# Depthwise convolution taps on TensorE for two output tokens at a time, in a two-block float32 transformer kernel

## The reference

```
q, k = rope(rms_norm(q)), rope(rms_norm(k))          # 8 heads of 64
attn = softmax(q @ k.T / 8, causal) @ v              # 256 tokens: one block
a, g = split(u + glu_b)
h    = pad(a * sigmoid(g), 30 rows in front)
conv[t, c] = sum_{j=0..30} dw_w[j, c] * h[t + j, c] + dw_b[c]     # 512 channels
conv = silu(layer_norm(conv) * ln_g + ln_b)
x    = x + concat(attn, conv) @ w_out
x    = x + (silu(h2 @ w_gate) * (h2 @ w_up)) @ w_down             # h2 = rms_norm(x)
```

## Time and profile before

| | us |
|---|---|
| median of three runs | 756.14 (755.87 to 756.16) |
| the profiled execution | 756.11 |
| its span in the trace | 754.3 |
| PE busy | 749.9, 99% of the span |
| DVE busy | 568.5, 75% |
| ACT busy | 400.9, 53% |
| POOL busy | 50.8, 7% |

### The profile page before, as it was taken

How to read it: one execution, slowest core, us unless ns; L and a number is a source line. 1 busy time by engine, 2 the same in 40 slices (tenths; PEclk the granted TensorE clock), 3 DMA queues, 4 the chain that set the end, 5 groups by cost and what they waited for, 6 DMA issues and landing times.

```text
span 754.3 us, 9798 instructions
## 1 busy us (share of the span) xinstructions
PE 749.9 (99%) x3820; PEld 620.8 (82%) x3820; DVE 568.5 (75%) x908; ACT 400.9 (53%) x524; POOL 50.8 (7%) x39
## 2 busy tenths in 40 slices
PE   9999999999999999999999999999999999999998
PEld 7888899888888888888888888887688888888887
DVE  6869789986767877687788748697658777768584
ACT  6765455646567546546555455655556344343430
POOL 0200000000002400000000000732000000000000
PEclk9999999999999999999999999999999999999999
DMA  9963434555363467565655575677034756565601
GB/s 313 386 221 95 157 120 161 195 169 162 117 219 116 167 212 261 182 219 175 218 179 178 200 222 206 227 188 271 2 113 147 244 179 211 171 210 177 222 3 56
DMA packets 71101, 137.12 MB, mean 182 GB/s; under 512 B 3216, under 2 KB 9232, under 8 KB 70928
## 3 DMA queue, kind: packets, MB, share of 16 engines
q1 hardware_dynamic: 70448, 136.37, 54.4%
q10 hardware_dynamic: 608, 0.14, 0.1%
HBM read 133.12 MB, written 1.05 MB: 178 GB/s over the span
## 4 chain that ended last, share of the span: by engine, by line
PE 95%; DVE 3%; ACT 1%; issue 1%; DVEq 0%; ACTq 0%
PE b L698 21%; PE b L700 21%; PE b L699 21%; PE SS L698 4%; PE SS L700 4%; PE SS L699 4%; PE TT L665 3%; PE OO L698 3%; PE OO L700 3%; PE OO L699 3%; DVE wlo L1668 1%; PE OO L1041 1%; PE b L871 1%; PE SS L817 1%; PE b L1041 1%; PE SS L835 1%
## 5 line engine op out<-in xcount | busy, mean ns | idle before, releaser
L1668 DVE TENSOR_TENSOR wlo<-raw,whi 128x2048 fp32r<-128x2048 f32 (+2 forms) x119 | 270.2, 2273 | 80.8 <-ACT whi L1205 80.1
L1205 ACT CAST whi<-raw 128x2048 fp32r<-128x2048 f32 (+2 forms) x119 | 222.9, 1878 | 124.3 <-PE b L700 85.9
L698 PE MATMUL b<-whi,Ahi 128*128 128x512 f32 (+2 forms) x520 | 204.0, 392 | 0.0
L700 PE MATMUL b<-whi,Alo 128*128 128x512 f32 (+2 forms) x520 | 199.5, 384 | 0.0
L699 PE MATMUL b<-wlo,Ahi 128*128 128x512 f32 (+2 forms) x520 | 199.3, 383 | 0.0
L700 PEld LDWEIGHTS b<-whi,Alo 128*128 128x128 f32 x520 | 97.9, 188 | 19.5
L698 PEld LDWEIGHTS b<-whi,Ahi 128*128 128x128 f32 x520 | 98.1, 189 | 18.6 <-ACT gates L1289 0.2
L699 PEld LDWEIGHTS b<-wlo,Ahi 128*128 128x128 f32 x520 | 98.1, 189 | 18.1
L2087 DVE STREAM_TRANSPOSE hT<-ust 32x256 f32<-32x256 f32 (+1 forms) x192 | 81.5, 425 | 2.7
L698 PE MATMUL b<-whi,Bhi 128*128 128x512 f32 x154 | 60.4, 392 | 0.1
L700 PE MATMUL b<-whi,Blo 128*128 128x512 f32 x154 | 60.0, 389 | 0.0
(11 more groups left out here) (311 smaller groups left out, 1023.2 us busy)
## 6 DMA issues: line engine op xcount, KB each, us to landing
raw<-in_w_in SPq DMA_DIRECT2D x38, 1024.0 KB, 5.1
raw<-in_w_up SPq DMA_DIRECT2D x16, 1024.0 KB, 5.4
raw<-in_w_dn SPq DMA_DIRECT2D x16, 1024.0 KB, 5.0
raw<-in_w_d SPq DMA_DIRECT2D x11, 1024.0 KB, 5.0
raw<-in_w_g SPq DMA_DIRECT2D x10, 1024.0 KB, 5.1
raw<-in_w_u SPq DMA_DIRECT2D x10, 1024.0 KB, 5.1
raw<-in_w_out SPq DMA_DIRECT2D x8, 1024.0 KB, 5.4
raw<-in_w_br SPq DMA_DIRECT2D x4, 1024.0 KB, 5.2
```

The lines of the kernel that those rows point to most:

```text
L698: e.matmul(dst, xh, H[:, kc, c0:ce], start=(first or c0 == 768) and kc == krs[0], stop=False)
L700: ins = e.matmul(dst, xl, H[:, kc, c0:ce], start=False, stop=last and kc == krs[-1])
L1205: e.copy(whi[:, s, 0:m], raw[:, r, 0:m]).then_inc(s_hi, 1)
L1668: e.tensor_tensor(wlo[:, s, 0:m], raw[:, r, 0:m], whi[:, s, 0:m].bitcast(F32), ALU.subtract).then_inc(s_lo, 1)
```

## The change

All taps go to PE, and a matmul makes two neighbouring output tokens at a time. The input `ch` is stored with even and odd tokens apart; `hs` has 8 shifts of 16 channels in its 128 partitions; a weight tile of 32 columns holds 16 channels for each of the 2 output phases; a matmul has 128 columns (token pairs). There are 8 outputs of 4 steps, 32 steps, 256 records. `hs` is filled through DRAM: 8 transfers of `ch` to an internal tensor, a wait for them, then 8 transfers of 140-element rows into `hs`. The second set stands one weight unit later in SP's list. DVE does no taps, and there are two `taps_out` of four outputs each. The attention's row sums come from a column of ones beside each head of V instead of `accum_out`; `aw` takes its reciprocals from the product's bank after it is done. `S2` has four buffers. The order of `az`, `ap`, tap steps and `at` stays. The layer norm has the token phases interleaved in each bank, so it takes four bn_stats of 256 elements and four subtract-multiplies of 256, and both turns back wait for all of them. Lists of steps: 6, then 9, 5, 5, 4, then 2, 1, 0.

```diff
-        tw = sb("tw", [128, 128 * len(TAPS)], c=r3)
-        hs = sb("hs", [128, 4 * NTE, 288], c=r3)
+        tw = sb("tw", [128, 4096], c=r3)
+        hs = sb("hs", [128, 8, 4, 144], c=r3)
...
-        ch = sb("ch", [128, 4, 288], c=g2)
+        ch = sb("ch", [128, 4, 2, 144], c=g2)
...
-        S2 = sb("S2", [128, 3, 384], c=g2)
-        V2 = sb("V2", [128, 2, 512], c=g2)
+        S2 = sb("S2", [128, 4, 384], c=g2)
+        V2 = sb("V2", [128, 2, 8, 72], c=g2)
...
+    shifts = nc.dram_tensor("shifts", [16, 8, 1152], F32, kind="Internal").ap()
...
             if i == unit_of["wo2", 0, 1, 0]:
                 w.wait_ge(s_ug, 2)
-                for g in range(4):
-                    for s in range(4):
-                        e.dma_start(hs[32 * s:32 * s + 32, NTE * g:NTE * g + NTE, 0:284],
-                                    ch[32 * g:32 * g + 32, :, s:s + 284]).then_inc(d_hs, 16)
+                for q in range(8):
+                    e.dma_start(shifts[:, q, :], ch[16 * q:16 * q + 16].rearrange("p k r u -> p (k r u)")).then_inc(d_ch, 16)
+            if i == unit_of["wo2", 0, 1, 0] + 1:
+                w.wait_ge(d_ch, 128)
+                for s in range(8):
+                    src = shifts.rearrange("c q (k r u) -> c (q k) r u", k=4, r=2)
+                    e.dma_start(hs[16 * s:16 * s + 16, :, :, 0:140].rearrange("p q k u -> p (q k) u"),
+                                src[:, :, s % 2, s // 2:s // 2 + 140]).then_inc(d_hs, 16)
             load(i)
...
         def conv(m):
-            o, j = TAPS[m]
-            bk, c = TAPB[o % 2], 256 * (o // 2)
+            o, j = m // 4, m % 4
+            bk, c = TAPB[o // 4], 128 * (o % 4)
...
             for g in range(4):
-                ins = e.matmul(bank[bk][32 * g:32 * g + 32, c:c + 256],
-                               tw[:, 32 * (4 * m + g):32 * (4 * m + g) + 32],
-                               hs[:, NTE * g + TILE[o], 4 * j:4 * j + 256], start=j == 0, stop=last)
+                ins = e.matmul(bank[bk][32 * g:32 * g + 32, c:c + 128], tw[:, 32 * (4 * m + g):32 * (4 * m + g) + 32],
+                               hs[:, 4 * (o % 2) + g, o // 2, 4 * j:4 * j + 128], start=j == 0, stop=j == 3)
...
-                        ins = e.matmul(bank[bk][64 * c:64 * c + 64, 128 * qb + 64 * i:128 * qb + 64 * i + 64],
-                                       PT2[:, i, a:a + 64], V2[:, kb, 64 * h:64 * h + 64], start=kb == 0, stop=kb == qb)
+                        o = 72 * (2 * qb + i)
+                        ins = e.matmul(bank[bk][64 * c:64 * c + 64, o:o + 65], PT2[:, i, a:a + 64], V2[:, kb, h, 0:65],
+                                       start=kb == 0, stop=kb == qb)
...
-        tile_parts(3)
+        tile_parts(6)
         for p in range(4):
             az(p)
             if p:
                 ap(p - 1)
-            tile_parts((7, 5, 5, 4)[p])
+            tile_parts((9, 5, 5, 4)[p])
             at(p)
         tile_parts(2)
         ap(3)
...
-        tile_parts(1)
+        tile_parts(0)
...
         def ln_turn(p):
             bk = NBK[p]
             clear(bk)
-            w.wait_ge(s_cf, NTE)
-            for k in range(4):
-                ins = e.transpose(bank[bk][:, 128 * k:128 * k + 128], cdv[:, k, 128 * p:128 * p + 128], ident)
-            ins.then_inc(s_l1, 1)
+            w.wait_ge(s_cf, p + 1)
+            turn4(bank[bk], cdv[:, 4 * p:4 * p + 4, :].rearrange("p o u -> p (o u)")).then_inc(s_l1, 1)
         def ln_back(p):
-            w.wait_ge(s_lv, p + 1)
+            w.wait_ge(s_lv, 2)
...
-            e.activation(P[:, 0:128], P[:, 0:128], ACT.Exp, bias=nm[:, 0:1], scale=-1.0, accum_out=l[:, 0:1])
-            e.activation(P[:, 128:384], P[:, 128:384], ACT.Exp, bias=nm[:, 1:2], scale=-1.0,
-                         accum_out=l[:, 1:2]).then_inc(s_ae, 1)
+            e.activation(P[:, 0:128], P[:, 0:128], ACT.Exp, bias=nm[:, 0:1], scale=-1.0)
+            e.activation(P[:, 128:384], P[:, 128:384], ACT.Exp, bias=nm[:, 1:2], scale=-1.0).then_inc(s_ae, 1)
...
+        def taps_out(b):
+            w.wait_ge(s_cp, b + 1)
+            e.tensor_tensor(cdv[:, 4 * b:4 * b + 4, :], bank[TAPB[b]].rearrange("p (o u) -> p o u", o=4),
+                            pcol("dw_b", 4 * b, 4).unsqueeze(2).broadcast_to([128, 4, 128]), ALU.add).then_inc(s_cf, 1)
...
         def aw(p):
-            w.wait_ge(s_ae, 2 * p + 2)
-            k = own(e.reciprocal(l, l))
+            o = bank[p % 2][:, 0:288].rearrange("p (q h d) -> p q h d", q=2, h=2)
+            l = sums[:, 4 * p:4 * p + 4].rearrange("p (q h) -> p q h", q=2)
+            w.wait_ge(s_ap, p + 1)
             w.wait_ge(s_ut, 4)
-            w.wait_ge(s_ap, p + 1)
+            k = own(e.reciprocal(l, o[:, :, :, 64]))
...
         for p in range(4):
             am(2 * p)
             am(2 * p + 1)
+            if p == 1:
+                taps_out(0)
             if p:
                 aw(p - 1)
-            conv((2, 2, 2, 2)[p])
-            if p in {1: 0, 2: 1, 3: 2}:
-                taps_out({1: 0, 2: 1, 3: 2}[p])
...
         def ln():
+            rows = [[bank[NBK[j]].rearrange("p (g r c) -> p r g c", r=2, c=16)[:, p] for j in range(2)] for p in range(2)]
+            for j in range(2):
+                w.wait_ge(s_l1, j + 1)
+                for p in range(2):
+                    k = own(e.bn_stats(bs[p][:, 6 * j:6 * j + 6], rows[p][j]))
             for p in range(2):
-                w.wait_ge(s_l1, p + 1)
-                k = own(e.bn_stats(bs[p], bank[NBK[p]]))
...
             for p in range(2):
                 w.wait_ge(s_rs, RS[f"l{p}"] + 1)
-                e.tensor_scalar(ys[:, p, 512:1024], bank[NBK[p]], mv[p][:, 0:1], lnr[p], ALU.subtract,
-                                ALU.mult).then_inc(s_lv, 1)
+                for j in range(2):
+                    ins = e.tensor_scalar(ys[:, p, 512 + 256 * j:768 + 256 * j].rearrange("p (g c) -> p g c", c=16),
+                                          rows[p][j], mv[p][:, 0:1], lnr[p], ALU.subtract, ALU.mult)
+                ins.then_inc(s_lv, 1)
```

More of the change, by code:

```diff
@@ L71 @@
       18: (33, 34, 35, 36), 20: (41, 42, 43, 44), 22: (45, 46, 47, 48)}
[L73 to L76, removed]
 CH2 = [(2048, 512), (1536, 512), (0, 512), (512, 512), (1024, 512)]
@@ L462, in build @@
     rp8, rpv, rpr = [stat(8) for _ in range(4)], [stat(8) for _ in range(4)], [stat(8) for _ in range(4)]
-    bs, mv, lnv, lnr = [[stat(n) for _ in range(2)] for n in (6, 2, 1, 1)]
+    mv, lnv, lnr = [[stat(n) for _ in range(2)] for n in (2, 1, 1)]
+    bs = [lscr[:, 16 * i:16 * i + 12] for i in range(2)]
     r1c, r1cq = rpv[3][:, 0:4:2], rpv[3][:, 1:4:2]
@@ L1030, in conv @@
         def conv(m):
-            o, j = TAPS[m]
-            bk, c = TAPB[o % 2], 256 * (o // 2)
+            o, j = m // 4, m % 4
+            bk, c = TAPB[o // 4], 128 * (o % 4)
             if m == 0:
-                w.wait_ge(d_hs, 256)
+                w.wait_ge(d_hs, 128)
                 w.wait_ge(d_tw, 32)
-            if j == 0:
+            if m % 16 == 0:
                 clear(bk)
-            last = (o, j + 1) not in TAPS
             for g in range(4):
-                ins = e.matmul(bank[bk][32 * g:32 * g + 32, c:c + 256],
-                               tw[:, 32 * (4 * m + g):32 * (4 * m + g) + 32],
-                               hs[:, NTE * g + TILE[o], 4 * j:4 * j + 256], start=j == 0, stop=last)
-            if last:
+                ins = e.matmul(bank[bk][32 * g:32 * g + 32, c:c + 128], tw[:, 32 * (4 * m + g):32 * (4 * m + g) + 32],
+                               hs[:, 4 * (o % 2) + g, o // 2, 4 * j:4 * j + 128], start=j == 0, stop=j == 3)
+            if m % 16 == 15:
                 ins.then_inc(s_cp, 1)
-                gone[bk] = (s_cf, o + 1)
+                gone[bk] = (s_cf, o // 4 + 1)
         def az(p):
@@ L2204, in ug @@
             for k in range(4):
+                ev = lambda a: a.rearrange("p (u r) -> p r u", r=2)
                 ins = e.scalar_tensor_tensor(
[L2206 to L2207 removed]
+                    out=ch[:, k, :, 15 + 64 * t:79 + 64 * t], in0=ev(src[:, 128 * k:128 * k + 128]),
+                    scalar=pcol("glu_b", k), in1=ev(ca[:, k, 128 * t:128 * t + 128]), op0=ALU.add, op1=ALU.mult)
             ins.then_inc(s_ug, 1)
[L2210 to L2237 removed]
+        def taps_out(b):
+            w.wait_ge(s_cp, b + 1)
+            e.tensor_tensor(cdv[:, 4 * b:4 * b + 4, :], bank[TAPB[b]].rearrange("p (o u) -> p o u", o=4),
+                            pcol("dw_b", 4 * b, 4).unsqueeze(2).broadcast_to([128, 4, 128]), ALU.add).then_inc(s_cf, 1)
         def am(h):
[L2240 removed]
+            Z, P = bank[3 + h % 2], S2[:, h % 4, :]
             nm = stat_m[h]
             w.wait_ge(s_az, h + 1)
[L2243 removed]
+            w.wait_ge(s_at, h - 3)
             w.wait_ge(s_dve, k_rn[1])
@@ L2299, in _ @@
         x_lo(("Y", 1, 0))
-        taps_out(3)
+        taps_out(1)
         def ln():
-            for p in range(2):
-                w.wait_ge(s_l1, p + 1)
```

(28 more changed lines are left out.)

79 lines of the change are left out of this document (22 added, 57 removed).

## The result

The changed kernel took 763.11 us (762.10 to 764.85, four runs), the kernel before 756.15 beside it; the ratio is 1.0095, with a 95% interval of 1.0075 to 1.0115. The forecast was 753.9, the range ended at 756.8. The profiled execution took 762.10, its span 760.3. The lines of the kernel's code stand one or two earlier than before (1041 is 1039, 1056 is 1053, 1079 is 1078, 665 is 664).

What follows compares the result with a forecast made beforehand. PE was taken to bound the stage, never stopping between the first tap block and the turn of `ys`; −3.20 there and +1.0 in the layer norm gave −2.2 us, from 756.11 to 753.9, range 752.8 to 756.8.

Steps and rivals of the forecast that it cites:

- The transfers: SP's queue filling `hs` through DRAM: transfer ends at 511.7, next weight unit lands at about 515, nothing added.
- Price of a row: Time per 560-byte row on each of 16 DMA engines in the transfer into `hs`; bounds 22 and 87 ns.
- I take 40: Chosen 40 ns per row into `hs`, as for small loads from DRAM (48 ns), not SBUF to SBUF.
- the 63 at which the sign turns: Row price in ns for `hs` at which the change's gain becomes a loss; no cost up to 54 ns.
- my upper bound of 87: Highest row price in ns, from old 1136-byte rows at 210 GB/s, SP's issuing included.
- The transfer is late: Rival: at 87 ns a row `hs` lands at 523.8, scores 7.9 us late at 530.3, total 761.8; chance 0.12.
- The tap steps: PE's tap matmuls: 29 ns a record plus 0.15 us per block; 48 records 1.54, 72 records 2.24.
- The rival in which they don't halve: Tap records bound by loads at 47 ns: +1.75 us, total 757.9; chance 0.12 for 35 to 47 ns.
- What PE meets in a pair: Attention pairs: PE's work 3.82 us, level with the exponentials' chain at 3.76 to 3.90; 3.90 taken, 4.14 with reads.
- The sum to the turn of `ys`: Stage from first tap block to the turn of `ys`: pieces together −3.20 us.
- The term of `aw`: `aw(3)` takes its reciprocal after the product: +0.28 us, fully on the path, since PE waits there for `ys`.
- The layer norm: Norm behind the stage, with four bn_stats and four subtract-multiplies: +1.0 us on the path, bounds +0.7 and +1.5.

Runs made afterwards that it cites:

- spread kernel: Changed kernel with each transfer into `hs` filling every eighth partition instead of 16 neighbours: 753.71 us, ratio 0.9969; with 18 KB rows as well, 753.4 us, ratio 0.9968.

## Why the prediction was wrong, and where it was right

**The step that failed is the one under "The transfers": "Price of a row", and in it "I take 40".** I put a row at 40 ns and so had nothing waiting for the transfer. From about 502, when the weight unit ahead was in, to the taps at 522.4 the transfer took some 20 us; 4096 rows over 16 engines are 256 each, so a row took 78 ns an engine (68 by the 131 GB/s of the windows alone). Both are beyond the 63 at which the sign turns, and below my upper bound of 87. (By the prediction's own numbers the wait begins at 56 ns and the sign turns near 64, not at its 54 and 63; the measured prices are beyond either.) The rival "The transfer is late" described what happened: `hs` at 522.4 (523.8 there), the unit at 524.85 (526.5), the scores at 528.38 (530.3). I gave it 0.12.

The size was in the bounds; the fault was in how I chose between them, and in the kind of price. I had taken the rate for a cost per row, and picked the row by where the data comes from. Both are refuted: 18 KB rows went at 120 to 129 GB/s, and 560-byte rows, from DRAM too, at 320. The evidence was in the earlier trace rows: 210 GB/s with the engines 0.91 busy, for transfers into 32 partitions, beside 398 for weights into 128. I had put the 210 down to SP's issue period. But at a busy share of 0.91 the DMA engines were hardly ever without work, which points to a limit inside the transfers, and the change halved the partitions of each. Scaling 210 by half would have given 105 GB/s and 22 us, and with it the late unit. That is a reading made afterwards; the old transfers also read from SBUF, and what the experiments show is the change of partitions alone.

**A second term was missing from the rival: the clock.** It has the scores 7.9 late and PE going on at full speed. In fact they were 6.0 late (0.8 of it the later start), and then they and the tap steps behind them ran at a granted 0.50 to 0.54: 72 tap records in 3.96 against 2.10 in the spread kernel, the eight scores in 1.65 against 0.86. That adds 2.65 us. The rival's 761.8 came out near the 763.1 by luck, with the lateness too large and the clock left out.

**The tap steps: right.** 48, 72, 40, 32 and 16 records took 1.45, 2.10, 1.23, 1.01 and 0.57, for 1.54, 2.24, 1.31, 1.08 and 0.61. With 0.15 per block off that is 27 ns a record, close to the lower bound of 26.7 and below the 29 that I took. The rival in which they don't halve falls.

**What PE meets in a pair: right, and shown.** 3.78 measured for 3.90, and 4.14 with the reads back, the turn's end computed for that case. As forecast the two sides are level. In pairs 1 and 2 of the spread kernel the pieces of PE alone fill the 3.78 (0.85, 0.85, 1.23 and 0.85), with no wait for ACT at a turn. In pair 3 PE has 0.22 less of taps, and the pair takes 3.79 all the same: there the loads of the turn wait for the exponentials.

```profile
PEld TT L665 <- ACT S L1554: 0.5, 2, 0.3
```

That the reads alone gain nothing without shorter taps was shown on the kernel before.

**The sum to the turn of `ys`**, read in the spread kernel, where no transfer disturbs it: first block +0.02 (+0.11 forecast), pair 0 −1.03 (−0.92), pairs 1 and 2 −2.06 (−1.81), pair 3 −0.58 (−0.47), the block behind −0.43 (−0.39), `aw` +0.18 (+0.28). Together −3.90 for −3.20; the 29 ns and the 3.90 were both a little high. The term of `aw` rested on a wait of PE for `ys` that the chain of the kernel before doesn't show: PE was at its last tap steps until the turn began.

```profile
543.02 0.57 PE b L1041 x8
```

The reciprocal itself took 0.21 start to start behind the product (538.64 to 538.85 in the spread kernel), for the 0.28 forecast.

**The layer norm: right.** In the changed kernel:

```profile
555.61 1.42 DVE L2279 BATCH_NORM_STATS2 st<-b 128x6 f32<-128x256 f32 x4
...
557.99 1.90 DVE L2288 TENSOR_SCALAR ys<-b,st 128x256 f32<-128x256 f32 x4 [0.36 <-POOL st L2370]
...
559.94 1.09 PE L664 MATMUL b<-cst,ys 128*128 128x128 f32 x8 [1.55 <-DVE ys L2288]
560.79 0.48 PE L697 MATMUL OO<-whi,Bhi 128*128 128x512 f32 x1
```

PE goes on 5.18 after the first bn_stats, for +4.06 before: +1.12, forecast +1.0. The subtract-multiplies began at +2.38, sooner than the 2.6 reckoned, and took 1.90 for some 1.68, so that they ended at +4.28, as forecast; two small misses cancel.

So with the layout changed the kernel takes 753.4 to 753.7, where 753.9 was forecast. That flatters the sum: the parts give −3.90 + 1.12 = −2.8 and the spread kernel measured −3.0, against a forecast of −2.2. (In the spread kernel's profile the stage also began 0.33 earlier, at 520.60.)

## What to carry to other kernels

Before a transfer is priced by its rows, ask which partitions each single transfer reaches on the SBUF side, and take the rate from a window of the trace with such a set; a DMA share near 1 at a low rate points to a limit inside the transfer. Where an operand's layout over the partitions is free, interleave what separate transfers write. A late transfer is charged to whoever stands in order behind it, here the copies of q and k behind a weight split whose own data was wanted only by the `wo2` products, from 550 on; and a cost that is hidden today (the accumulator reads) appears once the cover gets shorter, so parts that are worth nothing alone are measured together.

## What the runs showed of the hardware

- Transfers of 560-byte rows from DRAM into 16 partitions each: neighbours 98 to 138 GB/s, every eighth partition 179 to 208, and into all 128 at once 320 to 339. Rows of 18 KB into 16 neighbours: 124 over 504 to 520.
- In the changed kernel PE stood idle at a granted 1.00 from 523.95. The clock was 1.00 still over 524 to 526, 0.75 over 526 to 528, and 0.50 (1.2 GHz) over 528 to 532, with PE at work again from 528.4; it was 0.54 over 532 to 534 and 1.00 over 534 to 536. The wait of 0.71 us for `hs` left it at 1.00.
- A read of the accumulator lasts 0.18 to 0.19 us and costs about 0.10 start to start on ACT; four of them cost a pair 0.37 with the short taps and nothing with the long ones.
- What stays open: the `w_out` unit behind these transfers needed 13.6 us to land in one profiled execution (spread kernel, issued at 503.30) and 17.5 in another (with the reads, issued at 504.00), though the transfers ahead of it were the same. Those profiled with its split at 519.98, 521.64 and 521.55 took 754.64, 754.68 and 757.68 us, each 0.9 to 2.6 above its kernel's median (in the first the scores waited 1.0 us for ACT again); those with it at 516.8 and 516.9 took 751.64 and 753.13, at or just below theirs. Neither the layout nor the order of issue took this away, and no run tells what makes it differ.
